# GpSimd makes the high half of each weight piece by multiplying with one, in place of subtracting a broadcast zero

## The chip, the cores and the metric

The kernel runs on one core of one Trainium2 chip. The metric is the device time of one launch in microseconds (us). An execution under the hardware profiler gave the trace that is read here.

## What is computed

Four transformer layers over one sequence of 512 tokens with 1,024 channels, all in float32. The first two layers have the same form: a gated feed-forward block, a mixer (stick-breaking attention, latent attention and a short convolution side by side), a second gated feed-forward block, and a gated embedding. Layers three and four have a mixer (attention over selected keys, or over three dilated patterns, each beside attention over a memory) and one feed-forward block. So there are six feed-forward blocks in all, and they hold most of the multiplications:

```
def swiglu(x, w_gate, w_up, w_down):
    return (jax.nn.silu(x @ w_gate) * (x @ w_up)) @ w_down

for i in range(DEPTH):                      # DEPTH = 2
    h = rmsnorm(x, g_ffn1_pre[i])
    x = x + 0.5 * rmsnorm(swiglu(h, w1_gate[i], w1_up[i], w1_down[i]), g_ffn1_post[i])
    ...
```

The hidden width is 2,816, that is 22 tiles of 128.

## The kernel before

The activations lie in SBUF as 128 channels by 512 tokens, one tile for each 128 channels. TensorE has no full float32 multiplication in this kernel: every float32 number is cut into a high half, which is the number written as fp32r, and a low half, which is the number minus its high half. A product is then the sum of three matmuls: high weight by high activation, low weight by high activation, high weight by low activation (lines 461, 462 and 463, and 475 to 477 for the first two pieces of a stage).

**The weight stream.** All weights lie in device memory as one list of 554 pieces of 128 by 1,024 float32 (512 KB), in the order in which they are used. A piece is up to eight tiles of 128 by 128, and TensorE spends three matmuls with 512 moving columns on each tile, so 24 on a full piece. Three engines pass a piece on, each through two slots (j = 0 and 1):

- SyncE (line 374) loads a piece into raw[j] as soon as GpSimd has finished the piece that was in raw[j] before (semaphore w_split).
- GpSimd (function split) waits until the piece has landed and until TensorE has finished with the last piece in that slot (semaphore piece_used). Then it writes the high half WH[j] from raw[j] (line 393, semaphore w_hi), waits for that, and writes the low half WL[j] = raw[j] - WH[j] (line 395, semaphore w_split).
- TensorE waits for w_split and runs the piece (functions piece and first_pair), whose last matmul raises piece_used.

**The stages.** A feed-forward block has 44 full pieces for gate and up, and then 24 for the down projection: eight output chunks of 128 channels, each from three pieces of 8, 8 and 6 tiles. Because three pieces take turns in two slots, each chunk's pieces stand in slots 0, 1, 0 or 1, 0, 1. Each projection stage (there are twelve: six feed-forward blocks and six projections of a mixer or an embedding) starts with first_pair: its first two pieces are run together, tile by tile, as the normalised activation tiles become ready, so both slots come free at the same time, at its end. The third piece has to be split after that. Between stages GpSimd also sums squares (lines 412 and 414), with operations that the change leaves alone.

**The others.** In a gate and up stage VectorE takes the gate and up results out of PSUM (lines 1149 and 1151), multiplies them (line 1154) and makes the low half of the hidden activation (line 1157), and ScalarE has the sigmoid part (line 912) and the high half of the hidden activation (line 915) between them. The down projection starts when all hidden tiles are ready. Lines 1338 to 1345 are VectorE's angle tables for the rotations, and lines 1225 to 1229 the short convolution.

Of the kernel before, what the change touches and what calls it, by code (L numbers as in the profile page):

```python
# [7 lines left out]
P = 128  # L8
# [48 lines left out]
ALU, ACT, AX = mybir.AluOpType, mybir.ActivationFunctionType, mybir.AxisListType  # L57
# [54 lines left out]
def program(nc, A, trips):  # L112
# [11 lines left out]
    def sb(name, shape, dt=F32, offset=None):  # L124
        n = int(np.prod(shape[1:])) * (2 if dt == BF16 else 4)
        o = region(-(-n // 32) * 32) if offset is None else offset
        return nc.alloc_sbuf_tensor_at(name, list(shape), dt, offset=o)
# [6 lines left out]
    raw = sb("raw", [P, 2, TILES * P])  # L134
    WH = sb("WH", [P, 2, TILES * P], F32R)
# [19 lines left out]
    zero = sb("zero", [P, 1])  # L155
# [40 lines left out]
    def sem(name, start=0):  # L196
        credit[name] = start
        return ctx.enter_context(nc.semaphore(name))

    landed = [sem("w_landed0"), sem("w_landed1")]  # L200
    w_hi = sem("w_hi")
# [165 lines left out]
    @block.sync  # L367
    def _(sp):
        n = Counts(sp, credit, trips)
        with n.loop(PIECES // 2) as i:  # L370
            for j in range(2):

                sp.wait_ge(w_split, n.room(w_split))
                sp.dma_start(raw[:, j], A["w"][bass.ds(2 * i + j, 1)].rearrange("a p n -> p (a n)")).then_inc(landed[j], 16)
        for k in range(KD):
            sp.wait_ge(yb_ready, DEPTH * KD + k + 1)
            sp.dma_start(A["out"][k], Y[:, k]).then_inc(out_done, 16)
        sp.wait_ge(out_done, 16 * KD)

    @block.gpsimd  # L380
    def _(pool):
        n = Counts(pool, credit, trips)
        pool.sem_inc(w_split, 2)
        pool.memset(zero[:], 0.0).then_inc(w_hi, 1)
        pool.wait_ge(w_hi, n.full(w_hi))
        pool.sem_inc(xs_used, 2)

        def split(j, tiles):

            w = tiles * P  # L390
            pool.wait_ge(landed[j], n.full(landed[j], 16))
            pool.wait_ge(piece_used, n.room(piece_used))
            pool.tensor_tensor(WH[:, j, 0:w], raw[:, j, 0:w], zero[:, 0:1].broadcast_to([P, w]), ALU.subtract).then_inc(w_hi, 1)  # L393
            pool.wait_ge(w_hi, n.full(w_hi))
            pool.tensor_tensor(WL[:, j, 0:w], raw[:, j, 0:w], WH[:, j, 0:w], ALU.subtract).then_inc(w_split, 1)  # L395

        def split_all(pieces, tiles=TILES):
            with n.loop(pieces // 2):
                for j in range(2):
                    split(j, tiles)  # L400

        def first_two_and_squares(tiles=TILES):

            split(0, tiles)
            split(1, tiles)
            sum_squares()

        def sum_squares():
            for k in range(KD):
                pool.wait_ge(xs_ready, n.full(xs_ready))  # L410
                if k == 0:
                    ins = pool.tensor_tensor(XSS[:], SQ[:, 0], zero[:, 0:1].broadcast_to([P, S]), ALU.subtract)
                else:
                    ins = pool.tensor_tensor(XSS[:], XSS[:], SQ[:, k % 2], ALU.add)
                ins.then_inc(xs_used, 1)
                pool.wait_ge(xs_used, n.full(xs_used))

        def ffn():

            split_all(UP_PIECES - 2)  # L420
            with n.loop(KD // 2):
                for q in range(6):
                    split(q % 2, DOWN[q % 3])

        first_two_and_squares()
        with n.loop(DEPTH):
            ffn()
            first_two_and_squares()
            split_all(IN_A - 2)
            split_all(MH, KQ + KKV)  # L430
            split_all(KD)
            first_two_and_squares()
            ffn()

            split(0, TILES)
            split(1, TILES)
            first_two_and_squares()
            split_all(KD - 2)
            first_two_and_squares()
        for kind in ("dsa", "dil"):  # L440
            split_all((IN_DSA if kind == "dsa" else IN_DIL) - 2)
            split_all(4)
            split_all(KD if kind == "dsa" else KD // 2)
            first_two_and_squares()
            ffn()
            if kind == "dsa":
                first_two_and_squares()
            else:
                sum_squares()
# [1174 lines left out]
```

## Time and profile before

| | |
|---|---|
| median of 3 runs | 4055.58 us (4044.9 to 4061.43) |
| span of the profiled execution | 4054.8 us |
| TensorE busy | 3651.0 us, 90% |
| GpSimd busy | 2521.0 us, 62% |
| VectorE busy | 1623.3 us, 40% |
| ScalarE busy | 733.2 us, 18% |
| mean granted TensorE clock | 0.939 |
| loaded from device memory | 297.97 MB, 74 GB/s over the span |

The profile gives the span from the first to the last instruction and no other time for that execution; the span stands 0.8 us under the median of the three runs. TensorE's busy time comes from modelled ends of pipelined matmuls, so a matmul with 512 columns reads 0.39 us although the next one starts 0.23 us after it.

### The profile page before, as it was taken

The page shows a single profiled execution, that of the slowest core. Times are in us where ns is not written, and L with a number is a line of the kernel's source. Part 1 is how long each engine was busy: PE and PEld are TensorE (multiplying, and loading weights), DVE is VectorE, ACT ScalarE, POOL GpSimd, SP SyncE. Part 2 cuts the span into 40 slices and gives each one's busy share as a digit, 9 for nine tenths or more (in the row PEclk, how much of TensorE's full clock was granted, in tenths as well). Part 3 has the DMA queues.
Part 4 walks back from the last instruction along what each step waited for, and adds up shares of the span by engine and source line. Part 5 has one row for each costly group of instructions (what it writes and reads, how often), then busy time and mean ns, then how long its engine had stood idle before and what let it go on. Part 6 is the DMA issues. An engine that isn't in the chain of part 4 may idle for free.

```text
span 4054.8 us, 44758 instructions
## 1 busy us (share of the span) xinstructions
PE 3651.0 (90%) x15368; PEld 2798.1 (69%) x15368; DVE 1623.3 (40%) x2016; ACT 733.2 (18%) x1449; POOL 2521.0 (62%) x1217
## 2 busy tenths in 40 slices
PE   7999799799987999789989996789899989899998
PEld 5877565588765887665668774555688767667876
DVE  5430425444235441334354317785244124224420
ACT  2110123211022110113321113114211000222100
POOL 6877641578776887652368776540588776218876
PEclk9999898999998999998999998888999999879999
DMA  3222120122221222221122221210122222002222
GB/s 116 98 89 98 62 73 16 47 93 97 95 78 63 95 96 93 71 69 42 40 70 95 96 99 52 68 58 1 52 93 98 88 97 69 32 11 83 93 93 93
DMA packets 82895, 301.34 MB, mean 74 GB/s; under 512 B 9200, under 2 KB 9328, under 8 KB 82416
## 3 DMA queue, kind: packets, MB, share of 16 engines
q1 hardware_dynamic: 80928, 292.59, 21.6%
q10 hardware_dynamic: 1872, 7.51, 0.5%
q8 instruction: 56, 0.92, 0.1%
q14 instruction: 39, 0.32, 0.0%
HBM read 297.97 MB, written 2.10 MB: 74 GB/s over the span
## 4 chain that ended last, share of the span: by engine, by line
PE 70%; DVE 10%; POOL 10%; issue 6%; ACT 3%; DMA 1%; POOLq 0%; DVEq 0%; ACTq 0%; SPq 0%
PE psA L461 9%; PE psA L462 8%; PE psA L463 8%; PE psB L462 6%; PE psB L463 6%; PE psB L461 6%; PE psC L461 5%; PE psC L463 5%; PE psC L462 5%; POOL WL L395 4%; POOL WH L393 4%; PE psD L673 3%; DVE X L1118 3%; PE psB L648 2%; PE psA L648 2%
## 5 line engine op out<-in xcount | busy, mean ns | idle before, releaser
L393 POOL TENSOR_TENSOR WH<-raw,zero 128x1024 fp32r<-128x1024 f32 (+1 forms) x554 | 1023.0, 1847 | 1340.5 <-PE psC L463 879.6
L395 POOL TENSOR_TENSOR WL<-raw,WH 128x1024 fp32r<-128x1024 f32 (+1 forms) x554 | 1357.3, 2450 | 43.5
L461 PE MATMUL psA<-HH,WH 128*128 128x512 f32 x1632 | 657.2, 403 | 81.3 <-POOL WL L395 47.3
L462 PE MATMUL psA<-HH,WL 128*128 128x512 f32 x1632 | 647.4, 397 | 0.0
L463 PE MATMUL psA<-HL,WH 128*128 128x512 f32 x1632 | 646.8, 396 | 0.0
L461 PE MATMUL psC<-HIDH,WH 128*128 128x512 f32 x1056 | 422.3, 400 | 52.5 <-DVE HIDL L1157 35.1
L461 PEld LDWEIGHTS psA<-HH,WH 128*128 128x128 f32 x1632 | 314.4, 193 | 164.5 <-POOL WL L395 54.8
L463 PE MATMUL psC<-HIDL,WH 128*128 128x512 f32 x1056 | 419.5, 397 | 0.0
L462 PE MATMUL psC<-HIDH,WL 128*128 128x512 f32 x1056 | 418.7, 397 | 0.0
L461 PE MATMUL psB<-HH,WH 128*128 128x512 f32 x1008 | 394.7, 392 | 0.0
L463 PE MATMUL psB<-HL,WH 128*128 128x512 f32 x1008 | 392.2, 389 | 0.0
L462 PE MATMUL psB<-HH,WL 128*128 128x512 f32 x1008 | 392.2, 389 | 0.0
L462 PEld LDWEIGHTS psA<-HH,WL 128*128 128x128 f32 x1632 | 314.7, 193 | 67.4 <-issue 2.0
L463 PEld LDWEIGHTS psA<-HL,WH 128*128 128x128 f32 x1632 | 313.9, 192 | 67.4
L1151 DVE TENSOR_TENSOR Y<-psB,RS 128x512 f32<-128x512 f32 x132 | 91.2, 691 | 567.4 <-PE psB L463 567.4
L1141 DVE TENSOR_TENSOR YSS<-YSS,SQ 128x512 f32<-128x512 f32 x64 | 92.0, 1438 | 560.9 <-ACT SQ L937 546.1
L1157 DVE TENSOR_TENSOR HIDL<-Y,HIDH 128x512 f32 x132 | 232.4, 1761 | 130.1 <-ACT HIDH L915 130.1
L461 PEld LDWEIGHTS psC<-HIDH,WH 128*128 128x128 f32 x1056 | 201.4, 191 | 116.4 <-POOL WL L395 48.0
L915 ACT ACTIVATE HIDH<-Y 128x512 f32 x132 | 83.5, 632 | 828.1 <-DVE Y L1154 828.1
L462 PEld LDWEIGHTS psC<-HIDH,WL 128*128 128x128 f32 x1056 | 201.7, 191 | 44.2
L463 PEld LDWEIGHTS psC<-HIDL,WH 128*128 128x128 f32 x1056 | 201.5, 191 | 42.6
L1154 DVE TENSOR_TENSOR Y<-Y 128x512 f32<-128x512 f32 x132 | 214.1, 1622 | 23.6 <-DVE Y L1151 14.5
(238 smaller groups left out, 4581.6 us busy)
## 6 DMA issues: line engine op xcount, KB each, us to landing
raw<-in_w SPq DMA_DIRECT2D x554, 512.0 KB, 3.3
X<-in_x ACTq DMA_DIRECT2D x4, 512.0 KB, 8.0
NRAW<-in_mem ACTq DMA_DIRECT2D x2, 1024.0 KB, 5.1
out<-Y SPq DMA_DIRECT2D x8, 256.0 KB, 2.1
MRAW<-in_mask ACTq DMA_DIRECT2D x1, 1216.0 KB, 12.1
PRAW<-in_p ACTq DMA_DIRECT2D x2, 512.0 KB, 3.3
POSI<-in_pos ACTq DMA_DIRECT2D x2, 256.0 KB, 12.9
cf<-in_cf ACTq DMA_DIRECT2D x1, 384.0 KB, 4.9
```

The lines of the kernel that those rows point to most:

```text
L393: pool.tensor_tensor(WH[:, j, 0:w], raw[:, j, 0:w], zero[:, 0:1].broadcast_to([P, w]), ALU.subtract).then_inc(w_hi, 1)
L395: pool.tensor_tensor(WL[:, j, 0:w], raw[:, j, 0:w], WH[:, j, 0:w], ALU.subtract).then_inc(w_split, 1)
L461: pe.matmul(out, WH[:, slot, w], hi[:, t], start=start and t == 0, stop=False)
L462: pe.matmul(out, WL[:, slot, w], hi[:, t], start=False, stop=False)
L463: mm = pe.matmul(out, WH[:, slot, w], lo[:, t], start=False, stop=stop and t == tiles - 1)
L648: mm = pe.matmul(bank[:, at_key:at_key + w], qa, key, start=at_key % S == 0, stop=mask is None, skip_group_check=True)
L673: mm = pe.matmul(o, v, slot(PRT, i, deep)[:, b * P:(b + 1) * P], start=b == 0, stop=b == len(values) - 1, skip_group_check=True)
L1118: dve.tensor_tensor(X[:, k], X[:, k], T[:, k % 2], ALU.add).then_inc(x_ready, 1)
L1141: dve.tensor_tensor(YSS[:], YSS[:], SQ[:, j], ALU.add).then_inc(yss_step, 1)
L1151: dve.tensor_tensor(US[:, j], PB[:, j], RS[:], ALU.mult).then_inc(gu_free, 1)
L1154: dve.tensor_tensor(US[:, j], US[:, j], GS[:, j], ALU.mult).then_inc(hf_ready, 1)
L1157: dve.tensor_tensor(HIDL[:, m].rearrange("p a n -> p (a n)"), US[:, j], HIDH[:, m].rearrange("p a n -> p (a n)"), ALU.subtract).then_inc(h ...
```

## The change

In split, the high half is made by a tensor-by-scalar operation (raw times 1.0) with one tensor input, where before it was a tensor-by-tensor operation that subtracted a broadcast zero. A nop stands ahead of it. All 554 pieces go through this line; the low half's operation (line 395, which becomes 396) stays as it is.

```
             pool.wait_ge(landed[j], n.full(landed[j], 16))
             pool.wait_ge(piece_used, n.room(piece_used))
-            pool.tensor_tensor(WH[:, j, 0:w], raw[:, j, 0:w], zero[:, 0:1].broadcast_to([P, w]), ALU.subtract).then_inc(w_hi, 1)
+            pool.nop(nofuse=True)
+            pool.tensor_scalar(WH[:, j, 0:w], raw[:, j, 0:w], 1.0, None, ALU.mult).then_inc(w_hi, 1)
             pool.wait_ge(w_hi, n.full(w_hi))
             pool.tensor_tensor(WL[:, j, 0:w], raw[:, j, 0:w], WH[:, j, 0:w], ALU.subtract).then_inc(w_split, 1)
```

GpSimd's instructions in the loop over the down projection's chunks, one piece of 6 tiles and one of 8, before the change (a name in brackets is a semaphore waited for):

```order
L391 ISA
L393 TENSOR_TENSOR WH<-raw,zero 128x768 [waits piece_used,w_landed0]
L394 ISA
L395 TENSOR_TENSOR WL<-raw,WH 128x768 [waits w_hi]
L393 TENSOR_TENSOR WH<-raw,zero 128x1024 [waits piece_used,w_landed1]
L394 ISA
L395 TENSOR_TENSOR WL<-raw,WH 128x1024 [waits w_hi]
```

And the same place on GpSimd with the change:

```order
L391 ISA
L394 TENSOR_SCALAR WH<-raw 128x768 [waits w_landed0,piece_used]
L395 ISA
L396 TENSOR_TENSOR WL<-raw,WH 128x768 [waits w_hi]
L394 TENSOR_SCALAR WH<-raw 128x1024 [waits w_landed1,piece_used]
L395 ISA
L396 TENSOR_TENSOR WL<-raw,WH 128x1024 [waits w_hi]
```

Nothing has moved: the operation is another one, the same two semaphores are waited for ahead of it, and this list shows no row of its own for the nop. On the other engines the order is the same as before.

## Rows read from the trace of the kernel before

**Rows 1.** The page, parts 1 and 4: busy time by engine, and the chain that ended last.

```profile
span 4054.8 us, 44758 instructions
...
PE 3651.0 (90%) x15368; PEld 2798.1 (69%) x15368; DVE 1623.3 (40%) x2016; ACT 733.2 (18%) x1449; POOL 2521.0 (62%) x1217
...
PE 70%; DVE 10%; POOL 10%; issue 6%; ACT 3%; DMA 1%; POOLq 0%; DVEq 0%; ACTq 0%; SPq 0%
```

**Rows 2.** GpSimd's groups, shapes apart: busy us, mean ns, idle before.

```profile
L393 POOL TENSOR_TENSOR WH<-raw,zero 128x1024 fp32r<-128x1024 f32 x490 | 932.5, 1903 | 1123.9 <-PE psC L463 670.2 <-PE psA L463 295.3 <-PE psB L463 147.5
...
L393 POOL TENSOR_TENSOR WH<-raw,zero 128x640 fp32r<-128x640 f32 x16 | 20.0, 1253 | 102.4 <-PE psC L463 95.1 <-PE psA L463 7.2
```

**Rows 3.** Waits of TensorE for GpSimd: us in total, times, longest.

```profile
PE psA L461 <- POOL WL L395: 55.4, 19, 5.0
...
PE psC L461 <- POOL WL L395: 17.5, 42, 0.4
```

**Rows 4.** Time line, GpSimd, one chunk of the down projection: start us, us.

```profile
331.99 1.89 POOL L393 TENSOR_TENSOR WH<-raw,zero 128x1024 fp32r<-128x1024 f32 x1
333.96 2.73 POOL L395 TENSOR_TENSOR WL<-raw,WH 128x1024 fp32r<-128x1024 f32 x1
...
339.55 1.86 POOL L395 TENSOR_TENSOR WL<-raw,WH 128x768 fp32r<-128x768 f32 x1
343.43 1.90 POOL L393 TENSOR_TENSOR WH<-raw,zero 128x1024 fp32r<-128x1024 f32 x1 [2.02 <-PE psC L463]
```

**Rows 5.** Time line, TensorE, same stretch: matmuls that waited for GpSimd.

```profile
332.08 0.50 PE L461 MATMUL psC<-HIDH,WH 128*128 128x512 f32 x1 [0.44 <-POOL WL L395]
...
347.85 0.50 PE L461 MATMUL psC<-HIDH,WH 128*128 128x512 f32 x1 [0.38 <-POOL WL L395]
```

**Rows 6.** Chain of work in order of time, same stretch: start us, us.

```profile
336.86 3.32 DMA raw<-in_w
...
343.39 0.07 POOLq L394
...
345.40 2.40 POOL WL L395
...
348.35 0.23 PE psC L462
...
358.66 0.23 PE psC L462
```

**Rows 7.** Time line, TensorE: the first and last of 12 third pieces.

```profile
33.37 0.80 PE L461 MATMUL psA<-HH,WH 128*128 128x512 f32 x1 [5.02 <-POOL WL L395]
...
3673.38 0.79 PE L461 MATMUL psA<-HH,WH 128*128 128x512 f32 x1 [5.01 <-POOL WL L395]
```

**Rows 8.** Time line, TensorE: two of the 6 first pairs that waited.

```profile
14.52 0.77 PE L475 MATMUL psA<-HH,WH 128*128 128x512 f32 x1 [14.52 <-POOL WL L395]
...
1191.30 0.79 PE L475 MATMUL psB<-HH,WH 128*128 128x512 f32 x1 [5.02 <-POOL WL L395]
```

**Rows 9.** Time lines, VectorE and then GpSimd, in a gate and up loop.

```profile
158.36 1.67 DVE L1154 TENSOR_TENSOR Y<-Y 128x512 f32<-128x512 f32 x1 [0.19 <-DVE Y L1151]
...
157.58 1.89 POOL L393 TENSOR_TENSOR WH<-raw,zero 128x1024 fp32r<-128x1024 f32 x1 [1.13 <-PE psB L463]
159.56 2.73 POOL L395 TENSOR_TENSOR WL<-raw,WH 128x1024 fp32r<-128x1024 f32 x1
```

**Rows 10.** Time line, VectorE, the angle tables at the start.

```profile
29.07 2.05 DVE L1338 TENSOR_SCALAR T<-RY,VALL 128x512 f32<-128x512 f32 x1
...
40.36 0.43 DVE L1344 TENSOR_SCALAR T<-T 128x512 f32<-128x512 f32 x1
```

**Rows 11.** Groups, 60 to 270 us: a one-input row of ScalarE.

```profile
L915 ACT ACTIVATE HIDH<-Y 128x512 f32 x20 | 12.6, 632 | 130.4 <-DVE Y L1154 130.4
```

**Rows 12.** After two third pieces: us; busy PE, PEld, DVE, ACT, POOL; PEclk.

```profile
448.50:453.00 4.50, 4.50 (x20) 3.69 (x21) 0.00 (x0) 0.00 (x0) 4.14 (x2) 1.00 0.36 117
...
1294.70:1299.00 4.30, 4.30 (x10) 3.47 (x11) 0.00 (x0) 0.00 (x0) 4.13 (x2) 0.50 0.37 122
```

More of the change, by code:

```diff
@@ L392, in split @@
             pool.wait_ge(piece_used, n.room(piece_used))
-            pool.tensor_tensor(WH[:, j, 0:w], raw[:, j, 0:w], zero[:, 0:1].broadcast_to([P, w]), ALU.subtract).then_inc(w_hi, 1)
+            pool.nop(nofuse=True)
+            pool.tensor_scalar(WH[:, j, 0:w], raw[:, j, 0:w], 1.0, None, ALU.mult).then_inc(w_hi, 1)
             pool.wait_ge(w_hi, n.full(w_hi))
```

## The prediction, made before the changed kernel was run

> **What bounds the kernel now.** I read the page first. TensorE is busy 90% of a span of 4054.8 us, GpSimd 62%. The chain that ended last runs through TensorE for 70% and through GpSimd for 10% [rows 1]. So a faster GpSimd is worth something only where that chain passes through it. The groups of GpSimd say what the edited line costs: 1903 ns for 128x1024, 490 times, and 1253 ns for 128x640 [rows 2]. Beside it stand 1123.9 us in which GpSimd waited for TensorE to release a slot [rows 2]. Over most of the program GpSimd is ahead, and a shorter split there only lengthens its own wait.
>
> The view of waits then shows where TensorE waits for GpSimd. There are two kinds: 42 short waits in the down projection, and 19 in psA of up to 5.0 us each, 55.4 us together [rows 3].
>
> The short ones come from the piece with 6 tiles. TensorE runs it in 18 matmuls of about 0.229 us (from 348.35 to 358.66 us there are 45 of them [rows 6]), so 4.12 us. In that time GpSimd must split the next chunk's first piece, whose slot came free when the 6-tile piece began. That takes 1.90 + 0.08 + 2.40 us (343.43 to 347.8 [rows 4, 6]), and TensorE's matmul at 347.85 had to wait for it [rows 5]. The period of a chunk is 347.85 - 332.08 = 15.77 us [rows 5], while 66 matmuls need 66 x 0.229 = 15.11 us. So 0.66 us per chunk are lost to this.
>
> **The change, term by term.** Taken out: 554 subtractions. Put in: 554 multiplications by one and a nop each. Nothing is moved on any engine. One unknown decides the case, the duration of a one-input operation on GpSimd, which this trace never shows.
>
> Rows near it. The old operation grows by (1903 - 1253)/384 = 1.69 ns per element, with about 0.17 us fixed [rows 2]. The low half, which really reads two tensors, takes 2.40 us for 1024 elements and 1.86 us for 768, so 2.1 ns per element [rows 4, 6]. If one stream instead of two halves such a rate, 1024 elements cost 1.03 us (from 1.69) or 1.25 us (from 2.1). ScalarE does a one-input 512 in 632 ns, so 1.26 us for 1024 [rows 11]. VectorE does one in 0.43 us, so 0.86 us [rows 10]. The last two are other engines. I take **1.1 us**, which saves d = 0.8 us per split. The lower bound for the range is 0.86 us. The upper one is 2.40 us, the price of the low half, in case a tensor-by-scalar operation is a dearer program than the one it replaces.
>
> The Trainium skill, page "GPSIMD Engine Reference", section "Engine selection", calls a one-input operation on GpSimd "roughly line-rate"; at that page's 1.2 GHz, 1024 elements would be 0.85 us by an estimate from the page, plus the fixed part, so 1.02 us and a sum about 2 us better than mine. The same page speaks against that in "Performance pitfalls for Q7 kernels": packed reads there cost about 1.9 cycles per element, by an estimate 1.6 us plus the fixed part. That is my second case below. No row here settles between the two.
>
> The terms, with d = 0.8 us:
>
> 1. Down projections. The gap of a chunk is 0.66 us and d is larger, so all of it goes: 42 x 0.66 = **28 us**. The cover afterwards is 4.12 us of TensorE against 3.6 us of GpSimd. What is late next? Not the load: it lands at 336.86 + 3.32 = 340.18 us, and GpSimd then waits until 343.39 for the slot [rows 6].
> 2. Third pieces of a stage. After first_pair TensorE waits while one piece is split, 12 times, like 5.02 and 5.01 us [rows 7]. The wait holds one high half. 12 x 0.8 = **9.6 us**. The next split (3.6 us) then hides behind 24 matmuls (5.5 us).
> 3. First pairs that waited for GpSimd: 6. The one at 14.52 us holds two splits (1.6 us). The other five waited about 5 us and hold one high half each after the last slot came free [rows 8], so 5 x 0.8. Together **5.6 us**.
> 4. VectorE behind GpSimd. In a gate and up loop the multiplication asked at 158.36 us ended at 160.03, just after the high half had ended at 159.47 [rows 9]; the 0.56 us after that are about what such an operation needs by itself. So VectorE stands still while GpSimd holds something that both need. In the loop this is hidden behind TensorE. It counts at the end of each of six gate and up stages, where the down projection waits for the last hidden tile: with the high half ending 0.8 us sooner, the product and the last low half come about 0.6 us sooner. 6 x 0.6 = **3.6 us**. The Trainium skill, page "SBUF — State Buffer", section "Who interferes with whom", has this as an exclusive lock on a shared port; the trace agrees with 1.67 us for that multiplication.
> 5. VectorE's chains that TensorE waits for: the angle tables at the start, where an operation of 0.43 us took 2.05 us beside a high half [rows 10] and three such stand in a row with the splits, and, by my reading of the time line, the convolution in two layers with two each. That is 3 x 0.8 + 4 x 0.8 = 5.6 us, and with some 2 us in the projections of layers three and four I take **7.5 us**, an estimate.
> 6. The nop. A sequencer step on GpSimd's queue takes 0.07 us in the chain [rows 6]. It is exposed at the 18 places of terms 2 and 3, and within the spare 0.14 us at the 42: **-1.3 us**.
>
> Sum: 28 + 9.6 + 5.6 + 3.6 + 7.5 - 1.3 = 53 us. 4054.8 - 53 = 4001.8; the profiled span and the median of the runs differ by 0.8 us, so I say **4002 us**. One thing is left at nothing: after a third-piece wait of about 5 us TensorE is granted half its clock for a while (0.50 from 1294.70 to 1299 us against 1.00 from 448.50 to 453, 10 against 20 matmuls started in nearly the same time [rows 12]). Shorter waits may spare some of it; each time is worth about 10 x 0.2 = 2 us, and up to nine of the twelve could be hit. I put that into the lower end alone.
>
> **The rivals.**
>
> *Little is saved* (1.5 to 1.8 us instead of 1.1). For it: the cost may lie in the loop over elements and not in the second stream, since a broadcast operand hardly needs reading and still the old operation takes 1.69 ns per element. At 1.7 us, d = 0.2: 42 x 0.2 + 18 x 0.2 + 1.6 x 0.2 + 6 x 0.15 + 1.5 = 14 us less, minus the nop: 4042 us.
>
> *Nothing changes* (1.8 to 2.0 us): 4055 us. It is what happens too if the compiler's form of the operation runs the same loop as before.
>
> *Slower*, by one mechanism: the multiplication is dearer than the subtraction. At 2.40 us every place above loses 0.5 us: 42 x 0.5 + 19 x 0.5 + 6 x 0.5 + 4 = 38 us, so 4093 us. It decides from about 2.2 us on. From 2.7 us on it is worse, because split (2.7 + 0.1 + 2.73 [rows 4]) is then longer than TensorE's 24 x 0.229 = 5.5 us in every full piece, and each 0.1 us more costs some 50 us over the stream.
>
> *The gain is given back elsewhere*: GpSimd ends earlier, so the load starts earlier and VectorE's requests fall into the low half. Against it: loads have 3.2 us to spare, and the low half was there before. I hold it for a loss of a few us within my range.
>
> **How the numbers follow.** What a measurement of this kernel can tell from no change is about 0.5%, 20 us. That needs d of about 0.3 us, an operation under 1.6 us. Chances: as forecast 0.62 (0.86 to 1.4 us, which gives 3980 to 4018), little saved 0.17 (4018 to 4050, a little over half of it under 20 us), nothing 0.09, slower 0.12. Faster: 0.62 + 0.09 = 0.71; same: 0.08 + 0.09 + 0.01 = 0.18; slower 0.11. At the lower end: 0.86 us gives d = 1.04, 8 us more than the sum, and the clock up to 18 us more, so 3976 us. The upper end goes to 4050 us, which takes in the second case. The likeliest case alone is 3976 to 4020 us.
>
> **What the profile after would show.** The high half's group with a mean near 1.1 us, against 1903 ns. The 42 waits of psC for the low half gone and a chunk's period near 15.1 us. The twelve third-piece waits shorter by 0.7 to 0.8 us. GpSimd's wait for slots longer by some 554 x 0.8 us less what the span loses. VectorE's multiplication in the loop near 1.0 us. The prediction is wrong if the high half's mean is over 1.4 us, or if the 15.77 us period stays although the mean is short; then the gap is not GpSimd's split but something that TensorE's own queue does.

## The result and the profile after

The changed kernel took 4146.33 us (median of 4 runs, 4143.09 to 4151.68) against 4053.59 us for the kernel before (4 runs). The ratio is 1.0231 with a 95% interval of 1.0216 to 1.0247: the change costs 2.3%, about 93 us, where a gain of 53 us was forecast.

The page of the kernel after, its span, its busy times and its chain:

```profile
span 4145.2 us, 44967 instructions
...
PE 3688.5 (89%) x15354; PEld 2781.9 (67%) x15368; DVE 1345.0 (32%) x2016; ACT 733.1 (18%) x1449; POOL 2956.9 (71%) x1217
...
PE 61%; POOL 21%; DVE 8%; issue 5%; ACT 3%; POOLq 0%; DVEq 0%; DMA 0%; ACTq 0%; SPq 0%
```

GpSimd went from 2521.0 to 2956.9 us busy and from 10% to 21% of the chain that ended last, against [rows 1]. VectorE went the other way, from 1623.3 to 1345.0 us, with not one instruction of its own changed.

GpSimd's groups after, shapes apart:

```profile
L394 POOL TENSOR_SCALAR WH<-raw 128x1024 fp32r<-128x1024 f32 x490 | 1371.0, 2798 | 844.7 <-PE psC L464 589.0 <-PE psA L464 101.5 <-PE psB L464 84.2
L396 POOL TENSOR_TENSOR WL<-raw,WH 128x1024 fp32r<-128x1024 f32 x490 | 1204.5, 2458 | 40.9
...
L394 POOL TENSOR_SCALAR WH<-raw 128x640 fp32r<-128x640 f32 x16 | 29.0, 1810 | 90.3 <-PE psC L464 52.2 <-issue 33.1 <-PE psA L464 5.1
```

This is the whole surprise in one number: the operation with one tensor input takes 2798 ns, where the one with two took 1903 ns [rows 2]. It grows by (2798 - 1810)/384 = 2.57 ns per element, against 1.69 before.

TensorE's waits for GpSimd after:

```profile
PE psA L462 <- POOL WL L396: 71.5, 22, 6.6
PE psC L462 <- POOL WL L396: 55.2, 42, 1.3
...
PE psB L462 <- POOL WL L396: 29.6, 110, 0.4
```

The 42 waits of the down projection went from 17.5 to 55.2 us [rows 3], and a third line is new: 110 waits in the gate and up loops, where there was none. The time line of GpSimd in a down projection shows the first:

```profile
335.07 2.78 POOL L394 TENSOR_SCALAR WH<-raw 128x1024 fp32r<-128x1024 f32 x1 [1.42 <-PE psC L464]
337.93 2.37 POOL L396 TENSOR_TENSOR WL<-raw,WH 128x1024 fp32r<-128x1024 f32 x1
...
351.77 2.77 POOL L394 TENSOR_SCALAR WH<-raw 128x1024 fp32r<-128x1024 f32 x1 [1.43 <-PE psC L464]
```

A chunk's period is 351.77 - 335.07 = 16.70 us, against 15.77 [rows 5]. The new wait is seen in a gate and up loop, on TensorE first, then on GpSimd:

```profile
152.33 0.50 PE L462 MATMUL psB<-HH,WH 128*128 128x512 f32 x1 [0.28 <-POOL WL L396]
...
163.77 0.50 PE L462 MATMUL psB<-HH,WH 128*128 128x512 f32 x1 [0.25 <-POOL WL L396]
```

```profile
158.24 2.77 POOL L394 TENSOR_SCALAR WH<-raw 128x1024 fp32r<-128x1024 f32 x1 [0.74 <-PE psB L464]
161.09 2.63 POOL L396 TENSOR_TENSOR WL<-raw,WH 128x1024 fp32r<-128x1024 f32 x1
163.69 2.77 POOL L394 TENSOR_SCALAR WH<-raw 128x1024 fp32r<-128x1024 f32 x1
...
169.67 2.77 POOL L394 TENSOR_SCALAR WH<-raw 128x1024 fp32r<-128x1024 f32 x1 [0.73 <-PE psB L464]
```

From one split of a slot to the next it is 169.67 - 158.24 = 11.43 us, for two pieces that TensorE runs in 2 x 24 x 0.227 = 10.9 us. The kernel before needed just these 10.9 us, as its high half of 157.58 us [rows 9] and the next one in that slot show:

```profile
168.46 1.89 POOL L393 TENSOR_TENSOR WH<-raw,zero 128x1024 fp32r<-128x1024 f32 x1 [1.13 <-PE psB L463]
```

In one slot, split and piece alternate: GpSimd may write a slot only after TensorE has read it, and the other way round. 2.77 + 0.08 + 2.63 us of split and 5.45 us of piece make 10.93 us; the other 0.5 us pass at the two hand-overs (the wait for the semaphore, a slower first matmul, the end of the last one). Before, the same ring was 1.89 + 0.08 + 2.73 + 5.45 + 0.5 = 10.65 us by this estimate, so it was hidden behind the 10.9 us of TensorE; now it sets the pace.

VectorE's groups after show why it is less busy:

```profile
L1155 DVE TENSOR_TENSOR Y<-Y 128x512 f32<-128x512 f32 x132 | 126.0, 955 | 23.6 <-DVE Y L1152 14.5 <-ACT Y L913 3.8
...
L1158 DVE TENSOR_TENSOR HIDL<-Y,HIDH 128x512 f32 x132 | 92.8, 703 | 130.0 <-ACT HIDH L916 130.0
```

Before, the first took 1.67 us [rows 9], and the second 1761 ns by the group's mean. In a gate and up loop both start while the high half of 158.24 us is running, and the first ends in it too; the second ends at 161.47 us, 0.46 us after that high half. On VectorE's time line:

```profile
159.00 0.81 DVE L1155 TENSOR_TENSOR Y<-Y 128x512 f32<-128x512 f32 x1 [0.19 <-DVE Y L1152]
160.78 0.69 DVE L1158 TENSOR_TENSOR HIDL<-Y,HIDH 128x512 f32 x1 [0.96 <-ACT HIDH L916]
```

So the slow operation hardly blocks VectorE, unlike the subtraction. Over the whole time line, 120 of the 132 products (line 1155) run from start to end inside a one-operation high half, in 845 ns in the mean; beside no GpSimd operation one takes 0.69 us. Before, 124 of them started inside a subtraction and took 1.67 us in the mean, and none ended before it.

Where the loss sits can be read from the starts of TensorE's matmuls, stage by stage. The six gate and up loops, from the third piece on, took 1463.1 us in place of 1400.3, so 63 us more; 110 times the 0.55 us by which a pair of pieces grew make 61 of them. (The view of waits shows only 29.6 us of this. It counts a wait from the modelled end of the matmul before, 0.16 us after the next could have started, and the first matmul after a wait takes 0.11 us more.) The six down projections took 804.2 in place of 766.5 us, 38 us more, close to 42 times the 0.93 us by which a chunk's period grew. The six waits for the last hidden tile took 11.5 us less. Together that is 89 us, and the spans differ by 4145.2 - 4054.8 = 90.4 us. In all other places gains and losses nearly cancel: TensorE waits 24 us longer for GpSimd at psA and at the first pairs (71.5 - 55.4 and 46.9 - 39.4), and VectorE, less held up, gives back about as much in front of others, 12 us of it at the convolution (15.5 to 3.6) and 6 us at the start (10.1 to 3.7).

### The profile page after: what moved, and what is told of

Read it like the earlier page. It is cut to its first block, busy times and chain, and to the rows that moved or that the text cites. A ratio compares the mean times of both kernels' runs of the same rounds, so it can differ in the third digit from the quotient of the medians.

```text
span 4145.2 us, 44967 instructions
## 1 busy us (share of the span) xinstructions
PE 3688.5 (89%) x15354; PEld 2781.9 (67%) x15368; DVE 1345.0 (32%) x2016; ACT 733.1 (18%) x1449; POOL 2956.9 (71%) x1217
## 4 chain that ended last, share of the span: by engine, by line
PE 61%; POOL 21%; DVE 8%; issue 5%; ACT 3%; POOLq 0%; DVEq 0%; DMA 0%; ACTq 0%; SPq 0%
POOL WL L396 10%; POOL WH L394 10%; PE psC L462 7%; PE psC L464 7%; PE psC L463 7%; PE psB L462 6%; PE psB L464 6%; PE psB L463 6%; PE psA L462 4%; PE psA L463 3%; PE psA L464 3%; PE psD L674 3%; DVE X L1119 2%; PE psB L649 2%; PE psA L649 2%
## 5 line engine op out<-in xcount | busy, mean ns | idle before, releaser
L394 POOL TENSOR_SCALAR WH<-raw 128x1024 fp32r<-128x1024 f32 (+1 forms) x554 | 1502.3, 2712 | 1004.4 <-PE psC L464 710.5
L396 POOL TENSOR_TENSOR WL<-raw,WH 128x1024 fp32r<-128x1024 f32 (+1 forms) x554 | 1318.2, 2379 | 46.3
L462 PE MATMUL psC<-HIDH,WH 128*128 128x512 f32 x1056 | 422.3, 400 | 78.7 <-POOL WL L396 55.2
L462 PE MATMUL psB<-HH,WH 128*128 128x512 f32 x1008 | 409.2, 406 | 29.9 <-POOL WL L396 29.6
L462 PEld LDWEIGHTS psB<-HH,WH 128*128 128x128 f32 x1008 | 189.0, 187 | 117.2 <-POOL WL L396 80.0
L464 PEld LDWEIGHTS psB<-HL,WH 128*128 128x128 f32 x1008 | 189.2, 188 | 41.6
```

The source lines that it names most:

```text
L394: pool.tensor_scalar(WH[:, j, 0:w], raw[:, j, 0:w], 1.0, None, ALU.mult).then_inc(w_hi, 1)
L462: pe.matmul(out, WH[:, slot, w], hi[:, t], start=start and t == 0, stop=False)
L464: mm = pe.matmul(out, WH[:, slot, w], lo[:, t], start=False, stop=stop and t == tiles - 1)
```

## The experiments

Each is an edit of the kernel before at the line of the high half, unless it says otherwise. The kernel before was run beside them on the same chip.

**The nop alone.**

```
+            pool.nop(nofuse=True)
             pool.tensor_tensor(WH[:, j, 0:w], raw[:, j, 0:w], zero[:, 0:1].broadcast_to([P, w]), ALU.subtract).then_inc(w_hi, 1)
```

> The subtraction of before stays, and only the nop is put in ahead of it. Theory A (the multiplication is the dearer operation, 2.77 us against 1.90 for 1024 elements, and that is all of the 93 us lost): the nop costs a sequencer step, so 4053 to 4060 us, with the high half still at 1.89 us. Theory B (the nop, which takes the wait for a free slot away from the operation itself, delays each split): 4080 us or more, with longer idle times of GpSimd ahead of the high half.

Measured: 4059.25 us against 4055.63, ratio 1.0010 (0.9996 to 1.0025), the high half at 1904 ns. The nop isn't the cause; at most it costs a quarter of a per cent.

**Is it the form or the arithmetic?** Two edits: the one-input form with a subtraction, and the two-input form with a multiplication.

```
+            pool.nop(nofuse=True)
+            pool.tensor_scalar(WH[:, j, 0:w], raw[:, j, 0:w], 0.0, None, ALU.subtract).then_inc(w_hi, 1)
```

> A tensor-by-scalar operation that subtracts the constant 0.0, with the nop. Theory A1 (a tensor-by-scalar operation runs a dearer loop whatever its arithmetic): 2.77 us for the high half and 4146 us in all. Theory A2 (the multiplication is what is dear): about 1.9 us or less, and 4055 us or less.

```
+            pool.tensor_tensor(WH[:, j, 0:w], raw[:, j, 0:w], one[:, 0:1].broadcast_to([P, w]), ALU.mult).then_inc(w_hi, 1)
```

> A tensor-by-tensor operation that multiplies by a broadcast one, no nop. Theory A1 (the form of the operation sets its price, not the arithmetic): 1.90 us for the high half and 4053 us, as before. Theory A2 (multiplying is dear): near 2.8 us and 4146 us.

(The second kernel also sets `one` to 1.0 once, at the start; those lines are left out here.)

Measured: the first 4146.87 us, ratio 1.0231 (1.0200 to 1.0262), equal to the changed kernel; the second 4061.44 us, ratio 1.0016 (1.0000 to 1.0031), nearly the kernel before. Their rows of the high half, one kernel after the other:

```profile
L394 POOL TENSOR_SCALAR WH<-raw 128x1024 fp32r<-128x1024 f32 x490 | 1371.0, 2798 | 845.4 <-PE psC L464 589.3 <-PE psA L464 98.9 <-PE psB L464 84.6
```

```profile
L395 POOL TENSOR_TENSOR WH<-raw,one 128x1024 fp32r<-128x1024 f32 x490 | 933.6, 1905 | 1126.7 <-PE psC L465 673.4 <-PE psA L465 295.8 <-PE psB L465 147.6
```

The form sets the price and the arithmetic doesn't.

**A copy.** One input and no scalar.

```
+            pool.nop(nofuse=True)
+            pool.tensor_copy(WH[:, j, 0:w], raw[:, j, 0:w]).then_inc(w_hi, 1)
```

> A plain copy with one input and no scalar, with the nop. If a one-input operation can be cheap on GpSimd (my forecast had 1.1 us for 1024 elements), it is this one: about 1.1 us and 4000 us by the sum of the forecast. If every one-input operation runs the dearer loop: 2.8 us and 4146 us. I think a value in between the likeliest, 1.1 to 1.9 us.

Measured: 3993.34 us, ratio 0.9848 (0.9818 to 0.9879). The high half and TensorE's waits for GpSimd:

```profile
L394 POOL CAST WH<-raw 128x1024 fp32r<-128x1024 f32 x490 | 516.2, 1053 | 1493.1 <-PE psC L464 712.8 <-PE psA L464 426.5 <-PE psB L464 227.3
```

```profile
PE psA L462 <- POOL WL L396: 42.1, 17, 4.1
...
PE psB L476 <- POOL WL L396: 11.9, 3, 4.0
...
PE psA L476 <- POOL WL L396: 8.0, 2, 4.0
```

There is the price that the forecast gave to the multiplication, 1.05 us, and the 42 waits of psC are gone from the view. One-input operations are not all dear; the one chosen is.

**Two operations in place of one.** The same form as the change's, with a second operation that does nothing: first plus 0.0, then, to see whether the choice matters, times 1.0.

```
+            pool.tensor_scalar(WH[:, j, 0:w], raw[:, j, 0:w], 1.0, 0.0, ALU.mult, ALU.add).then_inc(w_hi, 1)
```

> Tensor-by-scalar with two operations, times 1.0 and plus 0.0. If the loop of that form always runs both stages, the price of the high half stays at 2.77 us and the time at 4146 us. If each stage costs, it is longer, 3.5 us or more, and the time above 4400 us.

```
+            pool.tensor_scalar(WH[:, j, 0:w], raw[:, j, 0:w], 1.0, 1.0, ALU.mult, ALU.mult).then_inc(w_hi, 1)
```

> Tensor-by-scalar with two multiplications by 1.0. If the presence of a second operation makes the form cheap, whatever the two are: 1.06 us for 1024 elements and 3995 to 4002 us. If it was the pair multiply and add that is cheap: 2.8 us and 4146 us.

Measured, in one run each: 4000.98 us and 3989.77 us, where the kernel before had 4051.49 and 4055.13. The high half in each:

```profile
L394 POOL TENSOR_SCALAR WH<-raw 128x1024 fp32r<-128x1024 f32 x490 | 521.3, 1064 | 1486.9 <-PE psC L464 709.1 <-PE psA L464 424.4 <-PE psB L464 224.9
```

```profile
L394 POOL TENSOR_SCALAR WH<-raw 128x1024 fp32r<-128x1024 f32 x490 | 522.8, 1067 | 1479.6 <-PE psC L464 709.7 <-PE psA L464 416.2 <-PE psB L464 225.0
```

Neither branch of the first expectation held. Of the second, the first branch did: 1067 ns, with a time 5 us under its range. The two kernels, alike in form and price, lie 11 us apart in one run each. Asking for more work made the operation 2.6 times faster: 1064 ns with two operations, 2798 ns with one. So the dear price belongs to the form with a second operation left empty.

**Is it the type of the output?** The one-operation multiplication only at the first step of each sum of squares, where input and output are both float32 (line 412).

```
-                    ins = pool.tensor_tensor(XSS[:], SQ[:, 0], zero[:, 0:1].broadcast_to([P, S]), ALU.subtract)
+                    pool.nop(nofuse=True)
+                    ins = pool.tensor_scalar(XSS[:], SQ[:, 0], 1.0, None, ALU.mult)
```

> The high half as before; the one-operation multiplication by 1.0 stands only at the first step of each sum of squares, 128x512 from float32 to float32. If the dear price belongs to the one-operation form, it takes about 0.2 + 512 x 2.5 ns = 1.45 us there. If it belongs to writing fp32r: about 0.6 us. The whole time hardly moves, 4045 to 4060 us.

Measured: 4056.54 us in one run. The row with the shortest, the middle and the longest duration in ns:

```profile
L413 POOL TENSOR_SCALAR YSS<-SQ x13: 1490/1927/2057, 13.9 to 4033.3; 128x512 f32<-128x512 f32 x13
```

The same row of the kernel before:

```profile
L412 POOL TENSOR_TENSOR YSS<-SQ,zero x13: 1039/1087/1485, 14.2 to 4033.1; 128x512 f32<-128x512 f32 x13
```

The shortest is 1490 ns for 512 elements, against an expected 1.45 us, and the subtraction there took 1039 at the shortest. Writing fp32r isn't the cause; the form is dear with float32 on both sides too.

**The price assumed, without the operation assumed.** The subtraction over 9/16 of the columns. This kernel leaves out a part of the result: the other 7/16 of the high half stay zero, as lines not shown here set them at the start.

```
+            v = w * 9 // 16
+            pool.tensor_tensor(WH[:, j, 0:v], raw[:, j, 0:v], zero[:, 0:1].broadcast_to([P, v]), ALU.subtract).then_inc(w_hi, 1)
```

> The subtraction of before, but over 9/16 of each piece's columns alone (576 of 1024), the rest of the high half being left as it was; so a part of the high half is left out. The operation should take 0.17 + 576 x 1.69 ns = 1.14 us, the price that the forecast assumed. If the forecast's sum over places was right and only the price was wrong: 4000 us, 3990 to 4012, with the 42 waits of psC for the low half nearly gone. Rival: the gain is not there even at that price, because the waits move to something else: 4030 us or more.

Measured: 3979.34 us (3974.64 to 3980.51) against 4051.49, ratio 0.9817 (0.9801 to 0.9833): 72 us faster. The high half, TensorE's waits, and the row in which VectorE sums squares in the down projection (here line 1144):

```profile
L396 POOL TENSOR_TENSOR WH<-raw,zero 128x576 fp32r<-128x576 f32 x490 | 570.7, 1165 | 1429.2 <-PE psC L466 741.2 <-PE psA L466 436.9 <-PE psB L466 241.7
```

```profile
PE psA L464 <- POOL WL L398: 41.4, 16, 4.3
...
PE psB L478 <- POOL WL L398: 12.5, 3, 4.2
...
PE psA L478 <- POOL WL L398: 8.3, 2, 4.1
```

```profile
327.54 0.69 DVE L1144 TENSOR_TENSOR YSS<-YSS,SQ 128x512 f32<-128x512 f32 x1 [14.42 <-ACT SQ L940]
```

At 1.17 us the places named in the forecast all gain, and the gain is larger than its sum. It also came out 10 us larger than the copy's (72 against 62 us, each against the kernel before beside it), though the copy is shorter; the intervals of the two ratios overlap, so this difference itself isn't shown. The copy's time line has one place where it loses, the same sum of squares:

```profile
326.95 2.89 DVE L1142 TENSOR_TENSOR YSS<-YSS,SQ 128x512 f32<-128x512 f32 x1 [12.21 <-ACT SQ L938]
```

With the copy, GpSimd's low half starts at 326.89 us, 0.06 us ahead of VectorE's sum, and VectorE stands behind all of its 2.41 us; with the shortened subtraction the sum starts at 327.54, 0.06 us ahead of the low half of 327.60, and it is the low half that takes 2.89 us. At the end of a down projection TensorE waits for this sum: 34.6 us in all with the copy, 21.0 with the shortened subtraction, 24.9 before. So the copy gives back 10 us there of what it gains elsewhere. That doesn't settle the difference between the two kernels: all waits of TensorE together are 346.8 us with the copy and 340.2 with the shortened subtraction, 7 us apart. Who comes first by 0.06 us can't be read from a price.

**Where the loss sits.** The multiplication and its nop in the gate and up loops alone (252 pieces), and in the down loops alone (144 pieces), by a flag handed to split.

```
-            split_all(UP_PIECES - 2)
+            split_all(UP_PIECES - 2, TILES, True)
```

> The multiplication with its nop only in the loops over gate and up pieces (252 of 554 pieces), the subtraction elsewhere. If split and piece alternate in a slot, a pair of pieces takes 11.44 us instead of 10.9: 20 pairs x 6 blocks x 0.55 = 66 us, six third pieces 5 us, less some 25 us that VectorE gets back at the start and at the ends of these stages: 4085 to 4115 us. Rival, that these loops stay hidden behind TensorE: 4050 to 4060 us.

```
-                    split(q % 2, DOWN[q % 3])
+                    split(q % 2, DOWN[q % 3], True)
```

> The multiplication with its nop only in the loops over down pieces (144 of 554 pieces). 42 waits that each grow by about 0.88 us, and 6 loops' first chunks in part: 4090 to 4098 us, a chunk's period of 16.7 us instead of 15.8. Rival, that most of the loss is elsewhere: under 4075 us.

Measured: 4125.63 us for the first, ratio 1.0180 (1.0163 to 1.0197), and 4076.69 us for the second, 1.0061 (1.0044 to 1.0078), both against 4051.49. So 74 and 25 us, 99 together, against 93 for the change. In the first, the view of waits has the new line and leaves the down projection nearly as it was; in the second it is the reverse:

```profile
PE psB L465 <- POOL WL L399: 29.8, 109, 0.4
...
PE psC L465 <- POOL WL L399: 18.6, 42, 0.8
```

```profile
PE psC L465 <- POOL WL L399: 56.1, 42, 1.7
```

The first came out 11 us above its range, since I counted 25 us back from VectorE at the start and at the ends of the stages; the waits for the last hidden tile stayed at 5.9 us in that kernel, and its gate and up loops took 64 us longer on TensorE's time line, near the 66 of the expectation. The second came out 13 us under. Its down projections took 37 us longer, but those waits fell to 3.9 us in that one, six times 1.9 us, and 37 - 11.5 = 25.6 us is what was measured. What VectorE gets back there depends on which operation GpSimd runs at that moment, and that is the first split of the down loop.

**Copies in both places.** As the copy above, and the first step of each sum of squares a copy too.

```
+                    pool.nop(nofuse=True)
+                    ins = pool.tensor_copy(XSS[:], SQ[:, 0])
```

> The plain copy for the high half, and also for the first of the eight steps of each sum of squares (13 times a subtraction of a broadcast zero over 512 columns, 1.2 us each). The copy of 512 columns should take about 0.6 us. If these stand on the path of the first pair in all 12 stages and at the end: 13 x 0.6 = 8 us less than with the high half's copy alone, 3985 us. If the sum waits for ScalarE's squares there, nothing: 3990 to 3996 us. I hold the second for likelier.

Measured: 3981.88 us (3979.39 to 3986.3) against 4055.13, ratio 0.9820 (0.9801 to 0.9840). That is 1.8% faster than the kernel before and 4.0% faster than the changed one (0.9820/1.0231 = 0.960, each ratio against the kernel before beside it). It leaves nothing out and is the version to keep. Whether the second copy itself is worth something stays open, and so does which branch of the expectation held, since 3981.88 us lies under both: the interval overlaps that of the high half's copy alone, the two were not run side by side, and the waits of TensorE are only 3 us shorter in all (343.8 against 346.8).

## Why the prediction was wrong, point by point

- **The price of the operation** is the step that failed: "I take 1.1 us". It measured 2.80 us. The bounds failed with it: the upper one was 2.40 us, the price of the low half where nothing held it up. All four rows that I compared were of other forms or other engines, and the real price lies above all of them. The argument was that one stream should cost half of two. A copy (1053 ns) and a multiplication with a second operation (1064 ns) show that it comes out for these two one-input forms; the form with one operation does not follow it, at 2.57 ns per element. Why an empty second operation costs that much isn't shown by any run.
- **The rival "slower"** had the direction and the cause of the price in part: the operation is dearer, though for its form and not for the multiplication. At 12% it was held too unlikely: nothing in the trace excluded it, since no row of that form was there. Its threshold for the full pieces, 2.7 us, was wrong. It compared one split with one piece (5.5 us), and by that comparison the measured split of 2.77 + 0.08 + 2.63 = 5.48 us would cost the gate and up loops nothing. They cost 63 us, because split and piece alternate in a slot and the hand-overs add 0.5 us. By an estimate from the same numbers that ring passes TensorE's 10.9 us once a split takes 10.9 - 5.45 - 0.5 = 4.95 us, so with a high half of about 2.2 us. The 4093 us given for 2.40 us lacks this term too.
- **"Each 0.1 us more costs some 50 us over the stream"** was not tested. In the ring, 0.1 us is paid once per pair of pieces and not per piece, so 277 x 0.1 = 28 us at most, an estimate.
- **The terms** were right in place, and this was tested apart from the price. At 1.17 us (the shortened subtraction) I would have forecast about 50 us of gain, and 72 came. Down projections: "all of it goes", 28 us; the 42 waits are gone, and the six stages took 766.5 - 736.3 = 30 us less. Third pieces: the twelve waits went from 47.3 to 38.3 us, so 0.75 us each, although only the two in [rows 7] were about 5 us long and the other ten stood at 3.2 to 4.6. First pairs: 39.4 us of waits for GpSimd became 20.8 us, with one of them, at the start, now waiting 13.2 us for ScalarE instead; net 5.4 us against 5.6 in the forecast. The last hidden tile: 35.1 to 30.6 us, 4.5 against 3.6. What is left, some 24 us, was to be the 7.5 us of VectorE's chains, of which the view of waits shows about 9 us (convolution 15.5 to 11.6, sums of squares 24.9 to 21.0, start 10.1 to 9.1). The rest, about 15 us, stays open. The clock, which I had left at nothing, explains little of it: the mean granted clock was 0.940 to 0.941 in the four runs and 0.939 to 0.942 in the seven of the kernel before beside them. With the two levels of the trace, 1.00 and 0.50, their means make about 473 and 480 us at the lower one, which is worth 4 us at most: an estimate, not an experiment.
- **A sign that came by luck.** "VectorE's multiplication in the loop near 1.0 us" came true (955 ns in the mean), but not because the high half ended sooner: it ended later, and held VectorE up less.
- **The nop**: -1.3 us was forecast, 3.6 us with an interval that takes in zero was measured.
- **"The gain is given back elsewhere"** came true in the kernel with the copy, as 10 us at VectorE's sum of squares (24.9 to 34.6), more than the "few us" that I gave it.

## What to carry to other kernels

The price of an operation that the trace doesn't show is a measurement and not an inference: a form with less work in it can run 2.6 times slower, and on GpSimd a copy, or a tensor-by-scalar operation with both operations given, is the cheap way to make a rounded copy. When an engine refills two slots behind another, don't compare its time for one slot with the other engine's time for one piece: add the two and the hand-overs, and compare the sum with the time of two pieces. Here that ring set the pace at a split of 5.48 us beside a piece of 5.45 us, and cost 0.55 us for each pair. Where two engines get in each other's way, the order of two starts that lie 0.06 us apart can decide which of them is held up (2.89 us or 0.69 us for the same sum).

## What was not expected of the hardware

- GpSimd, tensor-by-scalar over 128x1024 from float32 to fp32r: 2798 ns with one operation, 1064 to 1067 ns with two. A copy of the same shape takes 1053 ns, a tensor-by-tensor operation with a broadcast second input 1903 to 1905 ns.
- While the one-operation form runs on GpSimd, a VectorE operation with two inputs in SBUF is hardly held up: 845 ns in the mean for the 120 products that ran wholly inside one, against 1.67 us for the 124 that started inside the subtraction. It is not free of it altogether: the 50 sums of squares (line 1142) that ran wholly inside one took 1.21 us in the mean, where 0.69 us is the time alone. The Trainium skill, page "SBUF — State Buffer", section "Who interferes with whom", says that a VectorE instruction with two SBUF inputs contends with a GpSimd instruction that reads SBUF. The trace agrees for the tensor-by-tensor operations (2.89 us against 0.69) and not for this form, in which VectorE's operation isn't kept out until GpSimd's ends.
